# Rotary halves exchanged by transfers between on-chip buffers instead of a permutation product on TensorE

## The chip, the cores and the metric

The kernel runs on one core of a Trainium2 chip. The metric is the device time in microseconds of one execution. All inputs and the output are float32.

## The reference, cut to what matters

A two-layer encoder trunk over 512 frames of width 1024: multi-head latent attention (8 heads) with a gated ConvFFN, then an S5 state-space layer with a gated ConvFFN, and a final RMSNorm. The change concerns the rotary part of the attention only. The key has one rotary piece of 64 channels for all heads, the queries have one for each head. Each is split into halves of 32 channels and turned:

```python
def apply_rope(x, cos, sin):
    xf = x.astype(jnp.float32)
    x1, x2 = jnp.split(xf, 2, axis=-1)
    return jnp.concatenate([x1 * cos - x2 * sin, x1 * sin + x2 * cos], axis=-1).astype(x.dtype)
```

So every channel is multiplied by a cosine, its partner 32 channels away by plus or minus a sine, and the two are added.

## The kernel before, in words

**Layout.** Channels lie along the 128 partitions, the 512 frames along the free axis. A weight matrix is streamed in blocks of 128 output columns through two raw buffers (RAW) and split into a high and a low part (WH by ScalarE, `hi(b)`, L505; WL by VectorE, `lo(b)`, L862), so that each product is three matmuls (L1507 to L1509; L1649 to L1651 for values). Blocks are numbered: 0 to 5 the latent projection, 6 to 9 keys and values (ukv), 10 to 15 queries (uq), 16 to 23 the output projection (wo).

**Transfers of weights.** SyncE issues `load(b)` (L382 to L389) in order of b. `load(b)` first waits until `lo(b-2)` has read the raw buffer that it fills. SyncE's queue is in order, so everything written behind a load waits with it.

**Units.** The keys, values and queries are made in 28 units (`project(u)`, L1632), each a 128x512 tile in a bank of PSUM. Units 0 to 15 are key and value parts, 16 to 27 the queries in the order of QUNITS (L88): 16, 19, 22 and 25 hold rotary channels of two heads each, the others the plain channels of one head. Before a unit starts, its bank must have been read (`unit_free`, L1622; banks in UNIT_BANK, L91): unit 22 waits for the VectorE reading of unit 18, unit 25 for that of 21, unit 27 for that of 24. The readings are `unit_hi(u)` on ScalarE (L586) and, for keys and plain query units, `unit_lo(u)` on VectorE (L991).

**Rotation.** There are five turns, k = 0 for the key and 1 to 4 for the query pairs. The unturned tile lies in RAWR (the key's written by VectorE at L1017, a query pair's by ScalarE at L600). TensorE multiplies it by the signed permutation PERM (`permute(k)`, L1662 to L1670), and VectorE's `turned(k)` (L994) multiplies the product by SIN into TMP (L996), RAWR by COS (L997), and adds (L999). ScalarE then rounds the result (`key_rope_hi` L602, `rope_hi` L606) and VectorE takes the rest (`rope_lo` L1007). COS and SIN are spread over the partitions by `spread(0)` and `spread(1)` (TensorE L1589, ScalarE L541).

**Order.** The order of each engine is written out by hand. On TensorE, permute(0) stands between units 9 and 10, permute(1) to (3) behind units 17, 20 and 23, and permute(4) behind the scores of step 5 in the attention (L1743). VectorE's order around the turns (L1033 to L1049) is: unit_lo(12), turned(0), unit_lo(14), the key's rest, lo(11), lo(12), lo(13); unit_lo(17), turned(1), unit_lo(18), rope_lo(0); lo(14), unit_lo(20), turned(2), unit_lo(21), lo(15), rope_lo(1); unit_lo(23), turned(3), unit_lo(24); and then row_max(0), the attention's first step, with turned(4) in its step 10. The attention has 32 steps (8 heads by 4 query blocks): scores (TensorE), row_max (VectorE), exps (ScalarE), normalize (VectorE), turn (a transpose on TensorE), and pt_copy (ScalarE). ScalarE's exps(0) stands behind unit_hi(25), rope_hi(2) and hi(17).

Of the kernel before, what the change touches and what calls it, by code (L numbers as in the profile page):

```python
# [22 lines left out]
P = 128  # L23
# [30 lines left out]
ALU = mybir.AluOpType  # L54
ACT = mybir.ActivationFunctionType
# [15 lines left out]
FIRST = {}  # L71
# [18 lines left out]
NUNITS = 2 * HEADS + len(QUNITS)  # L90
UNIT_BANK = [(0, 1, 5)[_u % 3] for _u in range(18)] + [(4, 0, 1, 5)[_u % 4] for _u in range(8)] + [0, 1]  # L91

TURN_BANK = (6, 7, 6, 7, 1)


def unit_kind(u):
    if u < 2 * HEADS:
# [4 lines left out]
UNIT_READ = {}  # L102
# [56 lines left out]
for _b in FFN0:  # L159
    _p = PHASE_OF[_b]  # L160
    _rest = FIRST[_p] + BLOCKS[_p] - _b
    _ops = 3 if _p in ("dn00", "dn01") else 2 if _p == "dn02" else 0 if _rest <= 2 else 1
    OPS_AT[_b] = range(_i, min(_i + _ops, MAT_OPS * NJ))
    _i = OPS_AT[_b].stop
    for _o in OPS_AT[_b]:
        if _o % MAT_OPS == MAT_OPS // 2 - 1:
            SPILL_AT[_b + 5] = ("O", _o // MAT_OPS)
        if _o % MAT_OPS == MAT_OPS - 1:
            _n = max(_b + 3, FIRST["up00"])
            while _n - FIRST[PHASE_OF[_n]] < 2:  # L170
                _n += 1
            MAT_AT[_n] = _o // MAT_OPS
            SPILL_AT[_n + 6] = ("K", _o // MAT_OPS)
PLACE_FREE = {3: 1, 5: 2, 7: 4}
LAGS_AT = {1: 4, 3: 3, 4: 5, 6: 7}
assert _i == MAT_OPS * NJ and len(MAT_AT) == NJ and len(SPILL_AT) == 2 * NJ
# [5 lines left out]
def build(nc, d):  # L182
    ctx = ExitStack()
    with ctx:
# [8 lines left out]
        def keep(name, shape, dt=F32):  # L193
            t, base[0] = place(name, shape, dt, base[0])
            return t

        def sem(name):
            return ctx.enter_context(nc.semaphore(name))
# [15 lines left out]
        SQ = [keep(f"SQ{i}", [P, S]) for i in range(2)]  # L214
        DIAG = keep("DIAG", [P, TT, P])
        IDENT = keep("IDENT", [P, P])
        PERM = keep("PERM", [P, P])
        ONES = keep("ONES", [P, P])
        GAIN = keep("GAIN", [P, 5 * KD + KQ + KKV])
        CONV = keep("CONV", [P, DEPTH * 2 * NF, 4])  # L220
# [9 lines left out]
        DCOL = keep("DCOL", [P, KD])  # L230
# [27 lines left out]
        RAWR = [place(f"RAWR{i}", [P, S], F32, ah_at + 2048 * (5 + i))[0] for i in range(3)]  # L258
        TMP, COS, SIN = (place(n, [P, S], F32, al_at + 2048 * (5 + i))[0] for i, n in enumerate(("TMP", "COS", "SIN")))
        SEL, at = place("SEL", [P, TT, P], F32, ql_at)  # L260
# [68 lines left out]
        bank = [ctx.enter_context(nc.psum_tensor(f"bank{i}", [P, S], F32)) for i in range(8)]  # L329
# [7 lines left out]
        s_hi, s_lo, s_mm, s_ev = sem("w_hi"), sem("w_lo"), sem("block_done"), sem("bank_read")  # L337
# [4 lines left out]
        s_par, s_tab, s_pos, s_const = sem("gain_loaded"), sem("tables_loaded"), sem("pos_loaded"), sem("const_made")  # L342
        s_sml, s_ang, s_trig = sem("lambda_loaded"), sem("angles"), sem("trig")
        s_ra, s_cs, s_sel, s_csc = sem("rotary_angles"), sem("rotary_trig"), sem("trig_spread"), sem("trig_copied")
        s_tv, s_fb, s_un, s_uh = sem("latent_squares"), sem("factor_copied"), sem("unit_done"), sem("unit_hi")
        s_read = {"kq": sem("kq_read"), "v": sem("v_read"), "r": sem("rope_read")}
        s_rq, s_rh, s_qr = sem("rope_turned"), sem("rope_hi"), sem("rope_halves")
        s_den, s_b, s_bb, s_neg = sem("ssm_den"), sem("B_loaded"), sem("B_made"), sem("C_negated")
        s_pm, s_rot = sem("permuted"), sem("rotated")
        s_sc, s_mx, s_p, s_pn, s_pt, s_ptc, s_pv = (sem(n) for n in (  # L350
            "scores", "row_max", "exps", "probs", "probs_t", "probs_t_copied", "pv"))
        s_c, s_cv, s_sg, s_h = (sem(n) for n in ("tap2", "conv", "gate", "hidden"))
# [28 lines left out]
        def _(sp):  # L381
            def load(b):  # L382
                if b >= NBLOCKS:
                    return
                name = PHASE_OF[b]
                if b >= RW:
                    sp.wait_ge(s_lo, b - RW + 1)
                n = UNITS[name] * P
                sp.dma_start(RAW[b % RW][:, :n], d["w_" + name][b - FIRST[name]]).then_inc(s_raw[b % RW], 16)  # L389
# [11 lines left out]
            sp.dma_start(INV[:], d["inv"]).then_inc(s_pos, 16)  # L401
            for n in ("lr", "li", "ld"):
                sp.dma_start(small[n][:], d[n]).then_inc(s_sml, 16)
            for t, n in ((IDENT, "ident"), (SEL, "sel"), (PERM, "perm"), (CONV, "conv"), (DCOL, "dcol")):
                sp.dma_start(t[:], d[n]).then_inc(s_tab, 16)
            load(3)
            for t, n in ((CRE, "cre"), (CIN, "cim"), (MASK, "mask")):
# [6 lines left out]
            def lags(j):  # L414
                sp.wait_ge(s_kt, j + 1)
                sp.dma_start(KD_[j], KT[:]).then_inc(s_kw, 16)

            for b in range(4, FIRST["win"] + 4):
                load(b)
                if b == FIRST["wo"] + 5:  # L420
                    sp.wait_ge(s_pv, HEADS)
                    for t, n in ((BRE, "bre"), (BIM, "bim")):
                        sp.dma_start(t[:], d[n]).then_inc(s_b, 16)
                if b in SPILL_AT:
                    what, j = SPILL_AT[b]
                    if what == "O":
                        spill(j)
                    else:
                        lags(j)
# [63 lines left out]
        def _(act):  # L493
            act_ = nc.scalar.activation
# [45 lines left out]

            def spread(n, dst):  # L541
                act.wait_ge(s_sel, n + 1)
                act_(dst[:], bank[4][:], ACT.Copy).then_inc(s_csc, 1)

            hi(0)
            act.wait_ge(s_par, 16)
# [142 lines left out]
                if n == 4 * HEADS + 1:  # L689
                    o_hi(HEADS - 2)  # L690
            o_hi(HEADS - 1)
            act.wait_ge(s_tab, 16 * 5)

            def next_tile(key, kind, j, b):
                act.wait_ge(s_ev, nth(b))
# [144 lines left out]
            for i in range(KD):  # L840
                b = FIRST["glu"] + 2 * i + 1
# [12 lines left out]
        def _(dve):  # L854
            v = nc.vector
# [40 lines left out]

            v.memset(ONES[:], 1.0)
            v.memset(EPST[:], EPS)
            v.memset(WARM[:], 0.0).then_inc(s_const, 1)
            v.memset(KR2[0][64:128, :].bitcast(F32), 0.0)  # L900
            v.memset(KR2[1][0:64, :].bitcast(F32), 0.0)
# [52 lines left out]

            dve.wait_ge(s_sq, KD + KKV)
            v.tensor_tensor(SSKV[:], SQ[0][:], SQ[1][:], ALU.add).then_inc(s_ss, 2)
            dve.wait_ge(s_tab, 16 * 5)
            rstd_cols("x", RX)
            lo(4)
            dve.wait_ge(s_pos, 16 * 5)  # L960
# [31 lines left out]
                                ALU.subtract).then_inc(s_read["kq"], 1)  # L992

            def turned(k):  # L994
                dve.wait_ge(s_pm, k + 1)
                v.tensor_tensor(TMP[:], bank[TURN_BANK[k]][:], SIN[:], ALU.mult).then_inc(s_rot, 1)  # L996
                v.tensor_tensor(RAWR[k % 3][:], RAWR[k % 3][:], COS[:], ALU.mult)  # L997
                v.drain()
                v.tensor_tensor(RAWR[k % 3][:], RAWR[k % 3][:], TMP[:], ALU.add).then_inc(s_rq, 1)  # L999
# [501 lines left out]
        def _(pe):  # L1501
# [85 lines left out]
                    m.then_inc(s_mm, 1)  # L1587

            def spread(n):  # L1589
                pe.wait_ge(s_tab, 16 * 5)  # L1590
                pe.wait_ge(s_cs, n + 1)
                pe.wait_ge(s_ev, WA_READ[4])
                if n == 1:
                    pe.wait_ge(s_csc, 1)
                for c in range(TT):
                    m = mm(bank[4][:, c * P:(c + 1) * P], SEL[:, c, :], TRIG[n][:], start=True, stop=True)
                m.then_inc(s_sel, 1)
# [61 lines left out]
                        m = unit(b, KQ * (c % 2) + k, AH, AL, KKV + k, k == 0, k == KQ - 1, out)  # L1659
                m.then_inc(s_un, 1)  # L1660

            def permute(k):  # L1662
                pe.wait_ge(s_ev, (4, 5, 6, 6, 6)[k])
                if k >= 1:
                    pe.wait_ge(s_read["r"], k)
                if k in (2, 3):
                    pe.wait_ge(s_rot, k - 1)
                if k == 4:
                    pe.wait_ge(s_read["kq"], UNIT_READ[27][1])
                mm(bank[TURN_BANK[k]][:], PERM[:], RAWR[k % 3][:], start=True, stop=True).then_inc(s_pm, 1)  # L1670

            project(0)
            project(1)
            pe.wait_ge(s_fb, 2)
# [2 lines left out]
                project(u)  # L1677
            spread(0)
            project(9)
            permute(0)  # L1680
            project(10)
            spread(1)
            for u in range(11, 2 * HEADS):
# [1 line left out]
            for r in range(3):  # L1685
                project(2 * HEADS + 3 * r)
                project(2 * HEADS + 3 * r + 1)
                permute(r + 1)
                project(2 * HEADS + 3 * r + 2)
            project(25)  # L1690

# [20 lines left out]
            def turn(n):  # L1712
                qb = n % 4
                if n == 0:
                    pe.wait_ge(s_rot, 4)
                    pe.wait_ge(s_read["r"], UNIT_READ[25][1])
                pe.wait_ge(s_pn, n + 1)
                if n >= 3:
                    pe.wait_ge(s_ptc, n - 2)
                for kb in range(qb + 1):  # L1720
                    m = nc.tensor.transpose(bank[5 + n % 3][:, kb * P:(kb + 1) * P],
                                            PR_[qb][:, kb * P:(kb + 1) * P], IDENT[:])
                m.then_inc(s_pt, 1)

            def pv(h):
                pe.wait_ge(s_ptc, 4 * h + 4)
                if h == 0:
                    pe.wait_ge(s_read["v"], 2 * TT)
                if h == 1:
                    pe.wait_ge(s_rot, 5)  # L1730
                if h >= 2:
                    pe.wait_ge(s_act, TILE0["o"] + h - 1)
                for kb in range(TT):
                    m = mm(bank[h % 2][:, kb * P:], V[:, kb, h * VH:(h + 1) * VH], PT[h % 2][:, kb, kb * P:],
                           start=(kb == 0), stop=(kb == TT - 1))
                m.then_inc(s_pv, 1)

            pe.wait_ge(s_ev, 6)
            for n in range(4 * HEADS):
                scores(n)  # L1740
                if n in (0, 1):
                    project(26 + n)
                if n == 5:  # L1743
                    permute(4)
                if n >= 3:
                    turn(n - 3)
                if n >= 9 and n % 4 == 1:
                    pv((n - 9) // 4)
# [233 lines left out]
```

## Time and profile before

| what | value |
|---|---|
| median of 3 runs | 1143.05 us (1139.31 to 1145.65) |
| the profiled execution's own time | 1146.58 us |
| its span in the profile | 1144.8 us |
| mean granted TensorE clock | 0.987 |
| TensorE (PE) busy | 1116.7 us, 98% |
| VectorE (DVE) busy | 788.6 us, 69% |
| ScalarE (ACT) busy | 476.4 us, 42% |

The page of the profile gives busy times for the engines, the chain of work that ended last, the costliest groups of instructions, and the transfers with their time from issue to landing. In the timeline a matmul's start is exact and its end is modelled, so what a matmul costs is read from one start to the next. Positions are us from the start of the span. A table by stretch gives for each stretch its length, then busy us (and instructions) of PE, PEld (TensorE's weight loads), DVE, ACT and POOL, the granted TensorE clock (1.00 is full), the transfer engines' busy share, and GB/s. SPq is SyncE's sequencer, which issues transfers.

### The profile page before, as it was taken

How to read it: one execution, taken by the hardware profiler on the slowest of the kernel's cores; microseconds unless marked ns; L12 is line 12 of the kernel's file. 1: busy time of each engine (PE TensorE's matmuls, PEld its weight loads, DVE VectorE, ACT ScalarE, POOL GpSimd, SP SyncE). 2: the span in 40 equal slices, each digit the busy share in tenths (PEclk: the TensorE clock that was granted, in tenths of full speed). 3: DMA queues.
4: the chain of work that ended last, by engine and by line, in shares of the span. 5: the costliest groups of instructions: out<-in, count | busy, mean ns of one | idle time of the engine just before them, and what ended most of it. 6: DMA issues, size and time to landing. Idle time of an engine off the chain costs nothing.

```text
span 1144.8 us, 14849 instructions
## 1 busy us (share of the span) xinstructions
PE 1116.7 (98%) x5678; PEld 919.5 (80%) x5678; DVE 788.6 (69%) x1202; ACT 476.4 (42%) x721; POOL 57.9 (5%) x154
## 2 busy tenths in 40 slices
PE   8999899999999999999998999999999999999996
PEld 5787778888888888888887887888888888888885
DVE  6657857688787788978855885546765477635665
ACT  5556554455423543345451324334442244423442
POOL 3072004000000000000000000000000000000000
PEclk8999999999999999999998999999999999999998
DMA  6311103233343332433376663332333223232222
GB/s 210 102 59 52 37 20 111 78 114 126 106 130 111 116 123 92 148 111 120 89 260 202 175 186 93 94 109 75 109 95 108 93 92 95 90 111 92 93 78 87
DMA packets 62966, 125.68 MB, mean 110 GB/s; under 512 B 21808, under 2 KB 32560, under 8 KB 62896
## 3 DMA queue, kind: packets, MB, share of 16 engines
q1 hardware_dynamic: 61744, 120.54, 33.4%
q0 software_dynamic: 1152, 4.19, 1.1%
q8 instruction: 45, 0.74, 0.3%
q14 instruction: 25, 0.20, 0.1%
HBM read 110.04 MB, written 14.68 MB: 109 GB/s over the span
## 4 chain that ended last, share of the span: by engine, by line
PE 87%; DVE 5%; DMA 3%; DVEq 2%; ACT 1%; issue 1%; SPq 0%; ACTq 0%
PE bank L1507 27%; PE bank L1509 27%; PE bank L1508 27%; DVE MX L1057 1%; PE bank L1850 1%; DVE P L1065 1%; DVEq L1056 1%; PE bank L1799 1%; PE bank L1842 1%; DMA RAW<-in_w_wa 1%; ACT WH L505 1%; DMA RAW<-in_w_glu 1%; DVE WL L862 1%; DVE X L1289 1%; DMA ud_scratch<-UB 0%
## 5 line engine op out<-in xcount | busy, mean ns | idle before, releaser
L505 ACT ACTIVATE WH<-RAW 128x1024 fp32r<-128x1024 f32 (+1 forms) x184 | 190.0, 1034 | 392.2 <-PE bank L1509 352.6
L1507 PE MATMUL bank<-GH,WH 128*128 128x512 f32 x816 | 323.1, 396 | 3.2 <-DVE GL L920 3.2
L1508 PE MATMUL bank<-GL,WH 128*128 128x512 f32 x816 | 319.6, 392 | 0.0
L1509 PE MATMUL bank<-GH,WL 128*128 128x512 f32 x816 | 319.5, 392 | 0.0
L862 DVE TENSOR_TENSOR WL<-RAW,WH 128x1024 fp32r<-128x1024 f32 (+1 forms) x184 | 219.1, 1191 | 54.4 <-ACT WH L505 53.7
L1507 PE MATMUL bank<-AH,WH 128*128 128x512 f32 x596 | 235.2, 395 | 1.9 <-DVE WL L862 1.1
L1509 PE MATMUL bank<-AH,WL 128*128 128x512 f32 x596 | 232.2, 390 | 0.0
L1508 PE MATMUL bank<-AL,WH 128*128 128x512 f32 x596 | 232.0, 389 | 0.0
L1507 PEld LDWEIGHTS bank<-GH,WH 128*128 128x128 f32 x816 | 154.5, 189 | 36.7 <-DVE GL L920 4.1
L1509 PEld LDWEIGHTS bank<-GH,WL 128*128 128x128 f32 x816 | 154.5, 189 | 32.6
L1508 PEld LDWEIGHTS bank<-GL,WH 128*128 128x128 f32 x816 | 154.6, 189 | 32.4 <-issue 0.7
L1507 PEld LDWEIGHTS bank<-AH,WH 128*128 128x128 f32 x596 | 111.9, 188 | 27.2 <-DVE WL L862 1.5
L1508 PEld LDWEIGHTS bank<-AL,WH 128*128 128x128 f32 x596 | 111.9, 188 | 23.6 <-issue 1.0
L1509 PEld LDWEIGHTS bank<-AH,WL 128*128 128x128 f32 x596 | 111.9, 188 | 23.5
L771 ACT ACTIVATE CV<-Z,CONV 128x512 f32<-128x512 f32 x88 | 71.9, 817 | 94.0 <-DVE HH L1224 56.6
L1242 DVE SCALAR_TENSOR_TENSOR CV<-Z,CONV,CV 128x512 f32<-128x512 f32 x88 | 65.9, 749 | 41.6 <-ACT CV L771 41.6
L1235 DVE TENSOR_TENSOR Z<-bank,RSTD 128x512 f32<-128x512 f32 x88 | 60.5, 687 | 42.9 <-PE bank L1509 41.9
L1105 DVE TENSOR_TENSOR X<-bank,X 128x512 f32<-128x512 f32 x55 | 37.9, 688 | 58.0 <-PE bank L1509 58.0
L1245 DVE SCALAR_TENSOR_TENSOR CV<-Z,CONV,CV 128x512 f32<-128x512 f32 x88 | 66.1, 752 | 6.9 <-issue 0.4
L1228 DVE TENSOR_TENSOR AL<-HH,AH 128x512 fp32r<-128x512 f32 x44 | 30.2, 686 | 4.2 <-ACT AH L758 4.2
L754 ACT ACTIVATE SG<-CV 128x512 f32<-128x512 f32 x44 | 27.2, 618 | 12.1 <-DVE CV L1245 12.1
L1224 DVE TENSOR_TENSOR HH<-SG,CV 128x512 f32<-128x512 f32 x44 | 30.1, 685 | 0.2 <-ACT SG L754 0.2
(270 smaller groups left out, 930.9 us busy)
## 6 DMA issues: line engine op xcount, KB each, us to landing
RAW<-in_w_up SPq DMA_DIRECT2D x88, 512.0 KB, 3.5
RAW<-in_w_dn SPq DMA_DIRECT2D x32, 512.0 KB, 3.5
RAW<-in_w_glu SPq DMA_DIRECT2D x16, 512.0 KB, 3.5
RAW<-in_w_dn SPq DMA_DIRECT2D x16, 384.0 KB, 3.0
RAW<-in_w_wo SPq DMA_DIRECT2D x8, 512.0 KB, 3.5
od_scratch<-OO SPq DMA_DIRECT2D x8, 512.0 KB, 3.7
kd_scratch<-KT SPq DMA_DIRECT2D x8, 512.0 KB, 4.9
O<-od_scratch POOLq DMA_DIRECT2D x8, 512.0 KB, 4.5
```

Of the source, the lines that this page charges most:

```text
L505: act_(WH[b % RH][:, :n], RAW[b % RW][:, :n], ACT.Copy).then_inc(s_hi, 1)
L771: act_(CV[p][:], Z[p][:, 2:S + 2], ACT.Identity, scale=CONV[:, c, 2:3], bias=CONV[:, c, 3:4]).then_inc(s_c, 1)
L862: v.tensor_tensor(WL[b % RH][:, :n], RAW[b % RW][:, :n], WH[b % RH][:, :n].bitcast(F32), ALU.subtract).then_inc(s_lo, 1)
L1105: v.tensor_tensor(X[:, j, :], bank[BANK[b]][:], X[:, j, :], ALU.add).then_inc(s_ev, 1)
L1224: v.tensor_tensor(HH[:], SG[:], CV[0][:], ALU.mult).then_inc(s_h, 1)
L1228: v.tensor_tensor(AL[:, i, :], HH[:], AH[:, i, :].bitcast(F32), ALU.subtract).then_inc(s_act, 1)
L1235: v.tensor_tensor(Z[p][:, 2:S + 2], bank[BANK[b]][:], RSTD[:], ALU.mult).then_inc(s_ev, 1)
L1242: v.scalar_tensor_tensor(out=CV[p][:], in0=Z[p][:, 1:S + 1], scalar=CONV[:, c, 1:2], in1=CV[p][:], op0=ALU.mult, op1=ALU.add)
L1245: m = v.scalar_tensor_tensor(out=CV[p][:], in0=Z[p][:, 0:S], scalar=CONV[:, c, 0:1], in1=CV[p][:], op0=ALU.mult, op1=ALU.add)
L1507: mm(out, wh, hi_[:, k, :], start=start, stop=False)
L1508: mm(out, wh, lo_[:, k, :], start=False, stop=False)
L1509: return mm(out, wl, hi_[:, k, :], start=False, stop=stop)
```

## The change

PERM, its load and `permute` go. Instead SyncE exchanges the halves: `swap(k)` issues four transfers of 32 partitions by 512 elements (64 KB each) from RAWR to TMP, and VectorE's `turned(k)` waits for all four and multiplies TMP by SIN in place. The minus sign that PERM carried is put into SIN: `spread(1)` copies with a scale per partition from a new tile SIGN, filled by four memsets. `swap(0)` is issued behind load(12), `swap(1)` behind load(15), `swap(2)` behind load(16), `swap(3)` and `swap(4)` behind load(17). A swap waits until its RAWR is written and until the turn before it has ended with TMP. The scheduling waits that hung on the old semaphores are replaced by equivalent ones.

```diff
-TURN_BANK = (6, 7, 6, 7, 1)
+SWAP_AT = {FIRST["uq"] + 2: (0,), FIRST["uq"] + 5: (1,), FIRST["wo"]: (2,), FIRST["wo"] + 1: (3, 4)}
...
-        PERM = keep("PERM", [P, P])
+        SIGN = keep("SIGN", [P, 1])
...
+            def swap(k):
+                sp.wait_ge(s_ev, 6)
+                if k >= 1:
+                    sp.wait_ge(s_read["r"], k)
+                    sp.wait_ge(s_rq, k)
+                for r0 in range(0, P, 32):
+                    r1 = r0 + 32 if r0 % 64 == 0 else r0 - 32
+                    sp.dma_start(TMP[r0:r0 + 32, :], RAWR[k % 3][r1:r1 + 32, :]).then_inc(s_swp, 16)
+
             for b in range(4, FIRST["win"] + 4):
                 load(b)
+                if b in SWAP_AT:
+                    for k in SWAP_AT[b]:
+                        swap(k)
...
-                act_(dst[:], bank[4][:], ACT.Copy).then_inc(s_csc, 1)
+                if n == 0:
+                    act_(dst[:], bank[4][:], ACT.Copy).then_inc(s_csc, 1)
+                else:
+                    act_(dst[:], bank[4][:], ACT.Identity, scale=SIGN[:, 0:1]).then_inc(s_csc, 1)
...
+            for r0 in range(0, P, 32):
+                v.memset(SIGN[r0:r0 + 32, :], -1.0 if r0 % 64 == 0 else 1.0)
             v.memset(WARM[:], 0.0).then_inc(s_const, 1)
...
             def turned(k):
-                dve.wait_ge(s_pm, k + 1)
-                v.tensor_tensor(TMP[:], bank[TURN_BANK[k]][:], SIN[:], ALU.mult).then_inc(s_rot, 1)
+                dve.wait_ge(s_swp, 64 * (k + 1))
+                v.tensor_tensor(TMP[:], TMP[:], SIN[:], ALU.mult)
                 v.tensor_tensor(RAWR[k % 3][:], RAWR[k % 3][:], COS[:], ALU.mult)
...
-            def permute(k):
-                pe.wait_ge(s_ev, (4, 5, 6, 6, 6)[k])
...
-                mm(bank[TURN_BANK[k]][:], PERM[:], RAWR[k % 3][:], start=True, stop=True).then_inc(s_pm, 1)
...
-            permute(0)
...
-                permute(r + 1)
...
                 if n == 0:
-                    pe.wait_ge(s_rot, 4)
...
                 if h == 0:
                     pe.wait_ge(s_read["v"], 2 * TT)
+                    pe.wait_ge(s_read["kq"], UNIT_READ[26][1])
                 if h == 1:
-                    pe.wait_ge(s_rot, 5)
+                    pe.wait_ge(s_read["kq"], UNIT_READ[27][1])
...
-                if n == 5:
-                    permute(4)
```

## Rows read from the trace of the kernel before

**Rows 1.** The page: busy times, and the chain that ended last by engine

```profile
PE 1116.7 (98%) x5678; PEld 919.5 (80%) x5678; DVE 788.6 (69%) x1202; ACT 476.4 (42%) x721; POOL 57.9 (5%) x154
...
PE 87%; DVE 5%; DMA 3%; DVEq 2%; ACT 1%; issue 1%; SPq 0%; ACTq 0%
```

**Rows 2.** Table by stretch: projections with turns 1 to 3, then the attention's start

```profile
81.00:101.00 20.00, 20.00 (x85) 15.44 (x84) 15.97 (x24) 10.68 (x16) 9.97 (x24) 1.00 0.37 113
108.00:130.00 22.00, 18.52 (x99) 14.54 (x98) 17.70 (x56) 12.94 (x40) 0.00 (x0) 0.92 0.00 1
```

**Rows 3.** TensorE in order of time: start, us, around permute(1) and permute(4)

```profile
81.60 0.39 PE L1509 MATMUL bank<-AH,WL 128*128 128x512 f32 x1
81.83 1.02 PE L1670 MATMUL bank<-RAWR,PERM 128*128 128x512 f32 x2
...
82.92 0.40 PE L1508 MATMUL bank<-AL,WH 128*128 128x512 f32 x1
...
110.62 0.44 PE L1721 MATMUL bank<-IDENT,P 128*128 128x128 f32 x2 [1.61 <-DVE P L1065]
...
111.66 1.91 PE L1670 MATMUL bank<-RAWR,PERM 128*128 128x512 f32 x2
113.36 0.85 PE L1721 MATMUL bank<-IDENT,P 128*128 128x128 f32 x3
```

**Rows 4.** VectorE in order of time: the turns and what stands between them

```profile
75.18 0.68 DVE L996 TENSOR_TENSOR TMP<-bank,SIN 128x512 f32<-128x512 f32 x1
...
85.34 0.96 DVE L862 TENSOR_TENSOR WL<-RAW,WH 128x768 fp32r<-128x768 f32 x1 [2.95 <-ACT WH L505]
...
86.81 0.68 DVE L996 TENSOR_TENSOR TMP<-bank,SIN 128x512 f32<-128x512 f32 x1
...
88.17 0.69 DVE L999 TENSOR_TENSOR RAWR<-RAWR,TMP 128x512 f32<-128x512 f32 x1
...
93.09 0.68 DVE L996 TENSOR_TENSOR TMP<-bank,SIN 128x512 f32<-128x512 f32 x1
...
98.66 0.68 DVE L996 TENSOR_TENSOR TMP<-bank,SIN 128x512 f32<-128x512 f32 x1
...
101.63 0.11 DVE L1055 MEMSET bank<- 64x64 f32 x1 [0.33 <-PE bank L1710]
```

**Rows 5.** SyncE's queue in order of time: load(12), load(15), load(16), load(17), then spacing

```profile
68.42 0.33 SPq L389 DMA_DIRECT2D RAW<-in_w_uq  x1
...
86.32 0.33 SPq L389 DMA_DIRECT2D RAW<-in_w_uq  x1
...
92.60 0.33 SPq L389 DMA_DIRECT2D RAW<-in_w_wo  x1
...
96.63 0.33 SPq L389 DMA_DIRECT2D RAW<-in_w_wo  x1
...
7.91 1.99 SPq L400 DMA_DIRECT2D POSI<-in_pos  x4
```

**Rows 6.** Transfers by line: count, KB each, median us from issue to landing

```profile
out<-X SPq DMA_DIRECT2D x8, 256.0 KB, 2.3
PERM<-in_perm SPq DMA_DIRECT2D x1, 64.0 KB, 2.8
YB<-yd_scratch SPq DMA_DIRECT2D x8, 256.0 KB, 3.4
```

**Rows 7.** ScalarE in order of time: before the attention's first exponential

```profile
101.57 0.62 ACT L609 ACTIVATE QRS<-RAWR 64x512 fp32r<-64x512 f32 x1
...
105.22 0.37 ACT L654 ACTIVATE P<-bank,MX 128x128 f32<-128x128 f32 x1
```

**Rows 8.** Table by stretch: two stretches behind stalls of TensorE

```profile
111.30:114.70 3.40, 3.40 (x12) 2.26 (x11) 2.49 (x11) 2.39 (x9) 0.00 (x0) 0.50 0.03 7
...
618.40:626.70 8.30, 8.29 (x43) 7.21 (x44) 7.47 (x12) 2.40 (x5) 0.53 (x1) 0.50 0.55 162
```

**Rows 9.** TensorE in order of time: the stall ahead of the second stretch

```profile
618.41 1.97 PE L1850 MATMUL bank<-XR,O 64*128 64x64 f32 x16 [4.12 <-DVE XI L1340]
```

More of the change, by code:

```diff
@@ L348, in build @@
         s_den, s_b, s_bb, s_neg = sem("ssm_den"), sem("B_loaded"), sem("B_made"), sem("C_negated")
-        s_pm, s_rot = sem("permuted"), sem("rotated")
+        s_swp = sem("halves_swapped")
         s_sc, s_mx, s_p, s_pn, s_pt, s_ptc, s_pv = (sem(n) for n in (
@@ L403, in _ @@
                 sp.dma_start(small[n][:], d[n]).then_inc(s_sml, 16)
-            for t, n in ((IDENT, "ident"), (SEL, "sel"), (PERM, "perm"), (CONV, "conv"), (DCOL, "dcol")):
+            for t, n in ((IDENT, "ident"), (SEL, "sel"), (CONV, "conv"), (DCOL, "dcol")):
                 sp.dma_start(t[:], d[n]).then_inc(s_tab, 16)
@@ L691, in _ @@
             o_hi(HEADS - 1)
-            act.wait_ge(s_tab, 16 * 5)
+            act.wait_ge(s_tab, 16 * 4)
             def next_tile(key, kind, j, b):
@@ L956, in _ @@
             v.tensor_tensor(SSKV[:], SQ[0][:], SQ[1][:], ALU.add).then_inc(s_ss, 2)
-            dve.wait_ge(s_tab, 16 * 5)
+            dve.wait_ge(s_tab, 16 * 4)
             rstd_cols("x", RX)
@@ L1589, in spread @@
             def spread(n):
-                pe.wait_ge(s_tab, 16 * 5)
+                pe.wait_ge(s_tab, 16 * 4)
                 pe.wait_ge(s_cs, n + 1)
@@ L1660, in project @@
                 m.then_inc(s_un, 1)
-            def permute(k):
-                pe.wait_ge(s_ev, (4, 5, 6, 6, 6)[k])
[L1664 to L1669, printed above, removed]
-                mm(bank[TURN_BANK[k]][:], PERM[:], RAWR[k % 3][:], start=True, stop=True).then_inc(s_pm, 1)
             project(0)
@@ L1931 @@
     put("ident", np.eye(P, dtype=np.float32))
-    perm = np.zeros((P, P), np.float32)
-    for r in range(P):
-        o = r % 64
-        perm[r + 32 if o < 32 else r - 32, r] = -1.0 if o < 32 else 1.0
-    put("perm", perm)
     put("sel", (np.arange(P)[:, None, None] == np.arange(TT)[None, :, None] * 32 + np.arange(P)[None, None, :] % 32
```

## The prediction

> **What bounds the kernel now.** I read the page first: TensorE is busy 98% of the span and holds 87% of the chain that ended last [rows 1]. So a product taken off TensorE is worth its time only where TensorE has no gaps. The table by stretch shows which stage that is: from 81 to 101 us, where turns 1 to 3 stand, TensorE is busy 20.00 of 20.00 us, while from 108 to 130, in the attention, it is busy 18.52 of 22.00 and VectorE's 17.70 sets the pace [rows 2]. But from 85.34 to 101.2 VectorE is hardly idle either: its rows follow each other to the attention's first step at 101.63 [rows 4]. Two engines are nearly full here, and the change gives to one of them and puts a wait on the other.
>
> The sum is made against the profiled execution, 1146.58 us; the median of the runs is 1143.05. A difference of 0.5%, 5.7 us, is about what a measurement can tell from no change.
>
> **What is removed.** Permute(1) starts at 81.83 and the second matmul behind it at 82.92; with one ordinary matmul's 0.23 (81.60 to 81.83) taken off, it costs 0.86 us [rows 3]. Permutes 0 to 3 all stand in such a gapless stretch, so TensorE can be 0.87, 1.7, 2.6 and 3.4 us earlier, as far as nobody holds it up. Permute(4) takes 1.70 us (111.66 to 113.36), because the granted clock is half there [rows 3, 8], behind a stall of 1.61 us [rows 3]. It stands in the attention. What its removal returns there is between 0.3 us (VectorE sets the pace, and the product fills a gap) and 2.6 us (itself, and all the rest of what half clock costs in that stretch of 3.40 us, 1.7 us with the product's own 0.8). I take 1.9, since TensorE is busy all 3.40 us of it [rows 8]. The load of PERM stands far ahead of its use: nothing.
>
> **What is added at no cost.** The four memsets of SIGN delay the warm-up products by some 0.4 us; the first real products wait for inputs anyway. The copy to SIN stays one instruction, only with a scale, and turned(0), which needs it first, begins at 75.18, when units 10 to 13 have passed since. The product with SIN now reads TMP instead of a bank of PSUM; L999, which reads nothing from PSUM, took 0.69 us against 0.68 [rows 4]. Without these covers they would cost under 1 us together. Swap(0) is issued behind load(12), 68.42 [rows 5]; by the path below it lands at 73.0, and turned(0) is due at 75.18 - 0.87 = 74.3 [rows 4]: hidden, by 1.3 us. Swap(4) follows swap(3) by some 5 us and is used ten steps into the attention: hidden.
>
> **The path of a swap.** Four transfers, each a command for SyncE. POSI's four, also 32 partitions each, start (1.99 - 0.43) / 3 = 0.52 us apart, 0.43 being one of them [rows 5]. A load before it takes 0.40. From issue to landing no row shows a transfer from SBUF to SBUF. The nearest: 2.3 us (256 KB out of SBUF), 2.8 (64 KB from HBM, PERM itself), 3.4 (256 KB, read back) [rows 6]. I take 2.6, between the one that shares its source and the one that shares its size, and 2.3 and 3.4 as ends. So from the issue of the load ahead to VectorE seeing the data: 0.40 + 3 x 0.52 + 2.6 + 0.04 = 4.60 us.
>
> The Trainium skill ("DMA: Bandwidth & Descriptors", Anatomy of one DMA) gives about 2.0 us plus the bytes over 436 GB/s, 2.15 us for 64 KB, and says that the receipt from HBM is the slow part. An estimate by that page would lower the sum below by 3 x 0.45, to about +7.2. The rows here show nothing as short.
>
> **Where it is late.** The swaps stand in SyncE's queue behind loads, and load(b) is released by lo(b-2) on VectorE, which stands just ahead of the very turn that wants the swap. Load(15) is issued at 86.32 and turned(1) starts at 86.81, 0.49 later; load(16) 92.60 and turned(2) 93.09, 0.49 again; load(17) 96.63 and turned(3) 98.66, 2.03 later [rows 4, 5]. VectorE works in order, so it waits each time for the rest of 4.60 us:
> - turned(1): 4.60 - 0.49 = 4.11
> - turned(2): 4.60 - 0.49 = 4.11, because lo(14), behind turned(1), moves with it
> - turned(3): 4.60 - 2.03 = 2.57
>
> Together 10.8 us. VectorE's chain begins 0.87 earlier, since its step before followed TensorE, so turned(3) starts at 98.66 + 10.8 - 0.87 = 108.6. It takes 88.17 - 86.81 + 0.69 = 2.05 us [rows 4] and ends at 110.6. Behind it on VectorE are unit_lo(24) and the attention's first maximum; on ScalarE rope_hi(2), now at 101.57, and the first exponential, 3.65 later [rows 7]. ScalarE's part begins at 110.67 instead, so the attention starts **9.1 us later**. Three waits of TensorE follow from the same delays: unit 22 needs unit_lo(18), which ends at 86.81 + 4.11 - 0.87 + 2.05 + 0.7 = 92.8, while TensorE is there, 2.6 earlier than before, at 89.2 (stall 3.6). Worked out in the same way, unit 25 needs unit_lo(21), 103.1 (stall 4.2), and unit 27 needs unit_lo(24), 111.2 (2.8). The four products gained, 3.4 us, only make these stalls longer. They are not to be subtracted again.
>
> **The clock.** Stalls of 1.61 and 4.12 us had stretches of half clock, 3.4 us and 8.3 us of work, behind them [rows 3, 8, 9]. After these stalls I expect the same. Units 22 to 24 (27 matmuls of 0.23, 6.2 us) have 4 us of slack, so half clock there is nearly free. Half clock over units 25, 26 and the scores of steps 0 and 1 (5.3 us) can cost 2.5, and over the attention's first steps 1 to 3. Bounds 0 and 3.5; I take 1.3, somewhat below what the stretch of before costs.
>
> **Sum.** 9.1 - 1.9 + 1.3 = +8.5 us, so 1155.1 against the profiled 1146.58, and against the median **1151.5 us**. By its bounds: landing 2.3 to 3.4 (-0.9 to +2.4), spacing 0.40 as for a load (-1.1), permute(4) 0.3 to 2.6 and clock 0 to 3.5; not all at one end together, +5 to +13.5.
>
> **Rivals.**
> - *The clock stays half* from the first stall into the attention. Units 22 to 24 then run from 92.8 to 105.0, units 25, 26 and scores to 115.6; unit 27 starts 11.5 us late and is itself 2 longer; less 1.9 with the removed product, about +12, 1155. For it: 8.3 us in one stretch behind a stall of 4.12 [rows 8, 9], and three stalls here. Against: the stretch behind 1.61 was short. Chance 0.12.
> - *Short landing*: SBUF to SBUF in 1.5 us, below every row, and no half clock. Three waits lose 1.1 each: 9.1 - 3.3 - 1.9 = +3.9, 1147. For it: no HBM at either end. Against: 256 KB out of SBUF took 2.3. Chance 0.13.
> - *The transfers hide and TensorE's time comes back*: 3.4 for permutes 0 to 3 and 1.9 for permute(4), -5.3, 1137.7, faster. This decides only if a swap is at hand 0.49 us after the load ahead of it; the issue of four commands alone takes 1.6. Only a VectorE with slack that the rows don't show would let it happen. Chance 0.05.
> - That it doesn't do what it says I leave out: no product remains, and SIN carries the sign.
>
> The forecast (the three waits, +5 to +13.5) has 0.70.
>
> **Range and chances.** The forecast's own span, 1148 to 1156.5, is widened to take in the first rival and most of the second, and a microsecond of the measurement: **1146.5 to 1157.5**. Faster: the third rival, 0.05. Within 5.7 us: the short landing and the lowest part of the forecast, 0.17. Slower: 0.78.
>
> **What would show it.** VectorE idle before L996's successor three times, about 4.1, 4.1 and 2.6 us, released by the transfers into TMP, and hardly before turned(0) and turned(4). TensorE idle before units 22, 25 and 27, released by VectorE's L991. Load(16) and load(17) issued some 3 and 7 us later than now. First exponential near 114.3. The clock's table shows whether half clock lies in 90 to 120. I am wrong if VectorE's waits are below 1 us, if TensorE has no stall before unit 22, or if the attention starts late and a later stage takes it back.

## The result, and the profile after

The changed kernel took 1151.1 us (median of 4, 1149.98 to 1151.87) against 1142.24 us (median of 4), a ratio of 1.0078 with a 95% interval from 1.0060 to 1.0095: 8.9 us slower. The forecast was 1151.5, and +8.5 against the median known then, 1143.05; a fourth execution has since moved that median.

The page of the changed kernel, to be read beside [rows 1]:

```profile
PE 1114.6 (97%) x5668; PEld 919.1 (80%) x5668; DVE 789.0 (69%) x1206; ACT 476.7 (41%) x721; POOL 59.5 (5%) x154
...
PE 85%; DVE 6%; DMA 4%; DVEq 2%; ACT 1%; issue 1%; SPq 1%; ACTq 0%
```

TensorE has 2.1 us less work and a smaller share of a longer span. In the chain that ended last, VectorE, the transfers and SyncE's queue each have a point more.

VectorE in order of time, in the stage of the turns (beside [rows 4]). In brackets stands the idle time before an instruction, and what ended it:

```profile
79.31 0.97 DVE L876 TENSOR_TENSOR WL<-RAW,WH 128x768 fp32r<-128x768 f32 x1 [3.08 <-ACT WH L516]
80.20 0.68 DVE L1007 TENSOR_TENSOR QL<-bank,QH 128x512 fp32r<-128x512 f32 x1
84.68 0.69 DVE L1012 TENSOR_TENSOR TMP<-TMP,SIN 128x512 f32<-128x512 f32 x1 [3.80 <-DMA TMP<-RAWR]
...
95.64 0.69 DVE L1012 TENSOR_TENSOR TMP<-TMP,SIN 128x512 f32<-128x512 f32 x1 [4.53 <-DMA TMP<-RAWR]
...
104.27 0.69 DVE L1012 TENSOR_TENSOR TMP<-TMP,SIN 128x512 f32<-128x512 f32 x1 [2.96 <-DMA TMP<-RAWR]
```

Three waits, 11.3 us together, each ended by the transfers into TMP. The turns 0 (68.97) and 4 (127.16) start with no such wait. TensorE's stalls that follow from them, before units 22, 25 and 27:

```profile
87.46 0.50 PE L1523 MATMUL bank<-AH,WH 128*128 128x512 f32 x1 [3.51 <-DVE QL L1007]
...
98.36 0.80 PE L1523 MATMUL bank<-AH,WH 128*128 128x512 f32 x1 [2.87 <-DVE QL L1007]
...
106.98 0.50 PE L1523 MATMUL bank<-AH,WH 128*128 128x512 f32 x1 [1.60 <-DVE QL L1007]
```

SyncE's queue (beside [rows 5]): the weight load, and the four commands of a swap behind it.

```profile
80.31 0.33 SPq L388 DMA_DIRECT2D RAW<-in_w_uq  x1
80.76 2.42 SPq L424 DMA_DIRECT2D TMP<-RAWR  x4
90.55 0.33 SPq L388 DMA_DIRECT2D RAW<-in_w_wo  x1
90.99 2.41 SPq L424 DMA_DIRECT2D TMP<-RAWR  x4
99.20 0.33 SPq L388 DMA_DIRECT2D RAW<-in_w_wo  x1
```

Transfers by line (beside [rows 6]):

```profile
TMP<-RAWR SPq DMA_DIRECT2D x20, 64.0 KB, 2.6
```

From the issue of the load to VectorE's start the path is 84.68 - 80.31 = 4.37 us for turn 1, and 5.09 and 5.07 for turns 2 and 3. A single command takes 0.59 us, so they start (2.42 - 0.59) / 3 = 0.61 us apart.

**How the two profiles compare.** The profiled execution of before was a slow one: its fifth weight block is split 5 us later than in the changed kernel's, before anything that the change touches. So I compare stretches between two instructions that both kernels have. One is VectorE's split of the fifth weight block, `lo(4)`, ahead of all turns. The other is row_max(31), the attention's last. For before and for the changed kernel:

```profile
33.36 1.22 DVE L862 TENSOR_TENSOR WL<-RAW,WH 128x1024 fp32r<-128x1024 f32 x1
...
101.81 0.29 DVE L1057 TENSOR_REDUCE MX<-bank 128x1 f32<-128x128 f32 x1
...
161.60 0.69 DVE L1057 TENSOR_REDUCE MX<-bank 128x1 f32<-128x512 f32 x1
```

```profile
28.05 1.22 DVE L876 TENSOR_TENSOR WL<-RAW,WH 128x1024 fp32r<-128x1024 f32 x1
...
107.12 0.29 DVE L1073 TENSOR_REDUCE MX<-bank 128x1 f32<-128x128 f32 x1
...
165.40 0.69 DVE L1073 TENSOR_REDUCE MX<-bank 128x1 f32<-128x512 f32 x1
```

The stretch is 128.2 us before and 137.3 after: +9.1 us. Between lo(13) and row_max(0) alone it is +11.3 us (16.5 before, 27.8 after), as much as the three waits; 0.7 us come back ahead of lo(13) and 1.5 us behind row_max(0). The same stretches, from each run's timeline, in us (the runs are told below; the last column is the ratio of times to before, measured with each run):

| run | lo(4) at | lo(4) to row_max(31) | lo(13) to row_max(0) | ratio, 95% interval |
|---|---|---|---|---|
| before | 33.4 | 128.2 | 16.5 | 1 |
| before_again | 30.1 | 126.8 | 16.3 | 1.0002 (0.9989 to 1.0016) |
| changed | 28.1 | 137.3 | 27.8 | 1.0078 (1.0060 to 1.0095) |
| first_ahead | 28.2 | 135.1 | 24.2 | 1.0072 (1.0058 to 1.0087) |
| later_ahead | 28.1 | 130.1 | 20.5 | 1.0030 (1.0018 to 1.0042) |
| all_ahead | 31.9 | 127.5 | 16.8 | 1.0009 (0.9999 to 1.0018) |
| no_exchange | 28.0 | 126.4 | 16.6 | 1.0000 (0.9989 to 1.0011) |
| fill | 28.1 | 137.3 | 27.6 | 1.0082 (1.0060 to 1.0104) |
| eight_commands | 28.4 | 144.2 | 33.6 | 1.0144 (1.0111 to 1.0177) |
| best_order | 28.1 | 128.5 | 19.8 | 1.0010 (0.9996 to 1.0024) |
| before_lo | 28.7 | 128.2 | 17.5 | 1.0004 (0.9995 to 1.0014) |
| ahead_fill | 28.8 | 128.0 | 17.1 | 1.0000 (0.9990 to 1.0011) |
| ahead_lo | 28.8 | 125.1 | 17.0 | 0.9991 (0.9979 to 1.0003) |
| ahead_lo_again | 31.8 | 126.2 | 17.0 | 0.9983 (0.9970 to 0.9996) |

### The profile page after: what moved, and what is told of

Read it like the earlier page. It is cut to its first block, busy times and chain, and to the rows that moved or that the text cites. A ratio compares the mean times of both kernels' runs of the same rounds, so it can differ in the third digit from the quotient of the medians.

```text
span 1150.1 us, 14852 instructions
## 1 busy us (share of the span) xinstructions
PE 1114.6 (97%) x5668; PEld 919.1 (80%) x5668; DVE 789.0 (69%) x1206; ACT 476.7 (41%) x721; POOL 59.5 (5%) x154
## 4 chain that ended last, share of the span: by engine, by line
PE 85%; DVE 6%; DMA 4%; DVEq 2%; ACT 1%; issue 1%; SPq 1%; ACTq 0%
PE bank L1523 26%; PE bank L1525 26%; PE bank L1524 26%; DVE MX L1073 1%; PE bank L1852 1%; DVE WL L876 1%; DVE P L1081 1%; DMA ud_scratch<-UB 1%; PE bank L1801 1%; DMA TMP<-RAWR 1%; PE bank L1844 1%; ACT WH L516 1%; PE bank L1738 1%; DMA RAW<-in_w_glu 1%; DVE X L1305 1%
## 5 line engine op out<-in xcount | busy, mean ns | idle before, releaser
L1244 DVE TENSOR_TENSOR AL<-HH,AH 128x512 fp32r<-128x512 f32 x44 | 30.1, 685 | 4.2 <-ACT AH L772 4.2
L1240 DVE TENSOR_TENSOR HH<-SG,CV 128x512 f32<-128x512 f32 x44 | 30.1, 685 | 0.1
```

Source lines behind the costliest of these rows:

```text
L1240: v.tensor_tensor(HH[:], SG[:], CV[0][:], ALU.mult).then_inc(s_h, 1)
L1244: v.tensor_tensor(AL[:, i, :], HH[:], AH[:, i, :].bitcast(F32), ALU.subtract).then_inc(s_act, 1)
```

## The experiments

The theory: the loss is VectorE's three waits, and they are there because each swap stands in SyncE's queue behind a weight load that is released just ahead of the turn. The rivals: transfers and loads hinder each other, or half clock behind TensorE's stalls carries part of the loss.

**Swaps 1 to 3 one load earlier** (changed kernel, 11 executions).

```diff
-SWAP_AT = {FIRST["uq"] + 2: (0,), FIRST["uq"] + 5: (1,), FIRST["wo"]: (2,), FIRST["wo"] + 1: (3, 4)}
+SWAP_AT = {FIRST["uq"] + 2: (0,), FIRST["uq"] + 3: (1,), FIRST["uq"] + 5: (2,), FIRST["wo"]: (3,), FIRST["wo"] + 1: (4,)}
```

> The changed kernel with swap(1), swap(2) and swap(3) issued one load earlier (behind load(13), load(15) and load(16)), swap(4) behind load(17); nothing else changes. Theory (the loss is three waits of VectorE, because each swap stands in SyncE's queue behind a load that is released just ahead of the turn): VectorE's waits for the transfers fall from 3.8, 4.5 and 3.0 us to below 0.2, 0.2 and about 0.6, TensorE's stalls before units 22 and 25 go, and the time falls by 10 to 12 us against the changed kernel, to 1 to 4 us below the kernel before, 1138 to 1142. Rival (transfers and weight loads get in each other's way, wherever they stand in the queue, and the half clock behind the stalls carries part of the loss): the weight loads land later instead, and at least 4 us of the loss stay, 1146 or more.

Measured: 1141.93 us, ratio 1.0009 (0.9999 to 1.0018). The loss is gone: the time is 9.2 us below the changed kernel's. I had expected 10 to 12, and a time below the kernel before, which it isn't. VectorE waits before the turns only once:

```profile
98.02 0.69 DVE L1012 TENSOR_TENSOR TMP<-TMP,SIN 128x512 f32<-128x512 f32 x1 [0.37 <-DMA TMP<-RAWR]
```

TensorE's stall before unit 22 is down to 0.31 us, and those before units 25 and 27 are gone. The one wait that is longer than before is that of lo(13), for which the changed kernel waited 3.08 us:

```profile
84.03 0.96 DVE L876 TENSOR_TENSOR WL<-RAW,WH 128x768 fp32r<-128x768 f32 x1 [3.97 <-ACT WH L516]
```

Swap(1)'s four transfers are issued right behind load(13), and the block lands later. From the issue of load(13) to ScalarE's hi(13), here and in the run ahead_fill below, which differs only in the attention:

```profile
79.15 0.34 SPq L388 DMA_DIRECT2D RAW<-in_w_uq  x1
83.15 0.85 ACT L516 ACTIVATE WH<-RAW 128x768 fp32r<-128x768 f32 x1 [2.91 <-DMA RAW<-in_w_uq]
```

```profile
76.03 0.34 SPq L388 DMA_DIRECT2D RAW<-in_w_uq  x1
79.36 0.85 ACT L516 ACTIVATE WH<-RAW 128x768 fp32r<-128x768 f32 x1 [2.23 <-DMA RAW<-in_w_uq]
```

That is 4.0 us here and 3.3 there. It is 3.8 in first_ahead, 3.3 in both runs of ahead_lo, and 3.0 to 3.2 in the nine profiles in which no swap follows load(13). So the rival is right about 0.2 to 0.9 us of ten, and how much it is varies between executions of the same order.

**No exchange at all** (changed kernel, 12 executions; the rotary channels are multiplied by the sine without being exchanged).

```diff
-                if b in SWAP_AT:
-                    for k in SWAP_AT[b]:
-                        swap(k)
...
-                dve.wait_ge(s_swp, 64 * (k + 1))
-                v.tensor_tensor(TMP[:], TMP[:], SIN[:], ALU.mult)
+                if k >= 1:
+                    dve.wait_ge(s_read["r"], k)
+                v.tensor_tensor(TMP[:], RAWR[k % 3][:], SIN[:], ALU.mult)
```

> The changed kernel without the exchange: no swaps are issued, and turned(k) multiplies RAWR itself by SIN into TMP, so the rotary channels are not exchanged. It shows what the removed products are worth if their replacement costs nothing. Theory (3.4 us for permutes 0 to 3 on a full TensorE, and 0.3 to 2.6 us for permute(4)): 3.7 to 6 us below the kernel before, about 1137.5. Rival (VectorE, nearly full in this stage, is the bound, and the freed time of TensorE only lengthens its waits): less than 1.5 us below the kernel before.

Measured: 1141.4 us, ratio 1.0000 (0.9989 to 1.0011). The rival's answer: the removed products are worth less than 1.3 us, even if their replacement is free. VectorE's timeline shows why:

```profile
79.20 0.99 DVE L873 TENSOR_TENSOR WL<-RAW,WH 128x768 fp32r<-128x768 f32 x1 [3.06 <-ACT WH L513]
80.11 0.68 DVE L1004 TENSOR_TENSOR QL<-bank,QH 128x512 fp32r<-128x512 f32 x1
80.71 0.79 DVE L1010 TENSOR_TENSOR TMP<-RAWR,SIN 128x512 f32<-128x512 f32 x1
```

From lo(11) over load(13) to lo(13), and then through VectorE's full queue, runs a chain of its own: lo(11) to row_max(0) is 21.6 us here and 21.3 in both profiles of before. So TensorE, 20.00 of 20.00 us busy in [rows 2], was about as tight as that chain, and no tighter.

**The first swap alone, and the later two alone** (changed kernel, 4 and 9 executions).

```diff
+SWAP_AT = {FIRST["uq"] + 2: (0,), FIRST["uq"] + 3: (1,), FIRST["wo"]: (2,), FIRST["wo"] + 1: (3, 4)}
```

> The changed kernel with swap(1) alone issued earlier, behind load(13); swap(2) and swap(3) stay behind load(16) and load(17). Theory: the first wait of 3.8 us goes, the waits of 4.5 and 3.0 stay as long as they were; the time is 3.5 to 4.5 us below the changed kernel, 1146.5 to 1148. Rival (the slack ahead of the later turns is used up by the first wait, so that its removal comes back as longer later waits): within 1.5 us of the changed kernel.

```diff
+SWAP_AT = {FIRST["uq"] + 2: (0,), FIRST["uq"] + 5: (1, 2), FIRST["wo"]: (3,), FIRST["wo"] + 1: (4,)}
```

> The changed kernel with swap(2) and swap(3) issued earlier, behind load(15) and load(16); swap(1) stays behind load(15). Theory: the first wait stays at 3.8 us, the second falls to nearly nothing and the third to about 0.6; the time is 6 to 8 us below the changed kernel, 1143 to 1145. With the run that moves swap(1) alone the two savings add up to that of the run that moves all three, within 1.5 us. Rival (half clock behind the first stall is what makes the later ones long): a wait stays before turned(2) of over 2 us.

Measured: 1149.34 and 1144.79 us. The waits before the turns in the first run, and then in the second:

```profile
92.65 0.69 DVE L1012 TENSOR_TENSOR TMP<-TMP,SIN 128x512 f32<-128x512 f32 x1 [4.56 <-DMA TMP<-RAWR]
101.47 0.69 DVE L1012 TENSOR_TENSOR TMP<-TMP,SIN 128x512 f32<-128x512 f32 x1 [3.15 <-DMA TMP<-RAWR]
```

```profile
84.67 0.69 DVE L1012 TENSOR_TENSOR TMP<-TMP,SIN 128x512 f32<-128x512 f32 x1 [3.73 <-DMA TMP<-RAWR]
...
97.05 0.69 DVE L1012 TENSOR_TENSOR TMP<-TMP,SIN 128x512 f32<-128x512 f32 x1 [0.36 <-DMA TMP<-RAWR]
```

The waits behave as the theory says: each goes when its own swap moves, and the others stay. Between lo(13) and row_max(0) the first run saves 3.6 us and the second 7.3, together 10.9 of the 11.0 that moving all three saves. In the time, the second gives 6.3 us, as expected, and the first only 1.8 by the medians, half of what I expected (3.5 to 4.5). By its profile, 0.7 us of the difference is load(13), which lands later as in all_ahead, and 0.7 is the attention (59.0 us from row_max(0) to row_max(31) instead of 58.3), whose cause stays open. The 0.4 that are left are less than the intervals.

**The stalls of TensorE filled** (changed kernel, 6 executions).

```diff
+            def fill(n):
+                for _ in range(n):
+                    mm(bank[6][:], ONES[:], X[:, 0, :], start=True, stop=True)
...
+                if r == 2:
+                    fill(3)
...
+            fill(3)
             project(25)
...
+                    if n == 1:
+                        fill(1)
                     project(26 + n)
```

> The changed kernel with idle products on TensorE: three in float32 (0.86 us each) ahead of unit 22, three ahead of unit 25 and one ahead of unit 27, into a bank that nobody reads, so that TensorE is busy in most of its stalls. Theory (VectorE's waits set the time, and the stalls' half clock falls where TensorE has slack): within 1.5 us of the changed kernel, 1149.5 to 1151.5. Rival (half clock behind the stalls carries 2 us or more of the loss): 1148.5 or less, with no half clock between 85 and 105 us.

Measured: 1151.23 us. The changed kernel had these three stretches of half clock:

```profile
88.00:91.40 3.40, 3.40 (x9) 2.63 (x8) 2.93 (x4) 2.13 (x5) 0.00 (x0) 0.51 0.00 0
98.20:101.60 3.40, 3.24 (x8) 2.56 (x9) 3.03 (x5) 2.93 (x5) 0.00 (x0) 0.50 0.36 101
115.30:118.70 3.40, 3.28 (x14) 3.28 (x15) 2.93 (x12) 2.55 (x10) 0.00 (x0) 0.50 0.01 2
```

With the stalls filled the first two are gone, the third is there (115.5 to 118.9), and lo(4) to row_max(31) is 137.3 us in both. Half clock where TensorE waits for VectorE anyway costs nothing. The idle products don't fill the stalls to the end: 0.86, 1.83 and 1.71 us remain, the second of them here:

```profile
98.31 0.53 PE L1523 MATMUL bank<-AH,WH 128*128 128x512 f32 x1 [1.83 <-DVE QL L1007]
```

No half clock follows the last two, while it followed a stall of 1.61 us in [rows 3] and [rows 8]. The length of a stall alone doesn't decide it.

**Eight commands instead of four** (changed kernel, 4 executions).

```diff
-                for r0 in range(0, P, 32):
-                    r1 = r0 + 32 if r0 % 64 == 0 else r0 - 32
-                    sp.dma_start(TMP[r0:r0 + 32, :], RAWR[k % 3][r1:r1 + 32, :]).then_inc(s_swp, 16)
+                for r0 in range(0, P, 16):
+                    r1 = r0 + 32 if r0 % 64 < 32 else r0 - 32
+                    sp.dma_start(TMP[r0:r0 + 16, :], RAWR[k % 3][r1:r1 + 16, :]).then_inc(s_swp, 16)
...
-                dve.wait_ge(s_swp, 64 * (k + 1))
+                dve.wait_ge(s_swp, 128 * (k + 1))
```

> The changed kernel with each exchange issued as eight transfers of 16 partitions instead of four of 32. Bytes are the same, and four more commands stand in SyncE's queue per swap. Theory (the path of a swap is serial, and each command costs 0.63 us in it): each of the three waits grows by 2.5 us, and the time by 6.5 to 8.5 us against the changed kernel, 1157.5 to 1160. Rival (the landing of the bytes behind the weight load sets the wait, and the commands are hidden by it): the waits grow by less than 1 us each, 1154 or less.

Measured: 1157.52 us, ratio 1.0144. The waits:

```profile
70.26 0.69 DVE L1012 TENSOR_TENSOR TMP<-TMP,SIN 128x512 f32<-128x512 f32 x1 [0.88 <-DMA TMP<-RAWR]
88.39 0.69 DVE L1012 TENSOR_TENSOR TMP<-TMP,SIN 128x512 f32<-128x512 f32 x1 [6.20 <-DMA TMP<-RAWR]
100.98 0.69 DVE L1012 TENSOR_TENSOR TMP<-TMP,SIN 128x512 f32<-128x512 f32 x1 [6.22 <-DMA TMP<-RAWR]
111.29 0.69 DVE L1012 TENSOR_TENSOR TMP<-TMP,SIN 128x512 f32<-128x512 f32 x1 [4.64 <-DMA TMP<-RAWR]
```

They grow by 2.4, 1.7 and 1.7 us, the stretch by 6.9 and the time by 6.4 (expected: 2.5 each, and 6.5 to 8.5). The path is serial in SyncE's commands: in turns 1 to 3 the eight hold its queue for 4.93 us instead of 2.42. In turns 2 and 3 part of that comes back, because the last of eight is issued 2.5 us later behind the 512 KB load and lands in 2.0 us instead of 2.8. Turned(0), hidden in the changed kernel by about 1.6 us, now waits too.

**The kernel before once more** (10 executions, no edit).

> The kernel before, unchanged, profiled and timed once more. The profiled execution of before stood 5 us above the median, with a stall of TensorE of 2.3 us and 6.8 us of half clock at 12 to 19 us, which the profile of the changed kernel doesn't have. If these vary from execution to execution, this profile has them or not, and its execution time moves with them by about 5 us; if they belong to the kernel before, they are there again. The ratio should be 1 within 0.15%.

Measured: 1142.08 us, ratio 1.0002. In this profile lo(4) is at 30.08 instead of 33.36, and the half clock at the start is 3.4 us long instead of 6.8. In the other profiles lo(4) lies between 28.0 and 31.9, whatever the kernel. The start varies from execution to execution by up to 5 us. The half clock in the attention varies too: before had it, before_again not (58.4 us from row_max(0) to row_max(31) instead of 59.8), though TensorE's stall there is 1.61 us long in both.

**In search of a faster version.** Since the chain over load(13) holds the stage, lo(11), which releases it, was moved ahead of the key's rest:

```diff
             unit_lo(14)
-            key_rope_lo()
             lo(11)
+            key_rope_lo()
             lo(12)
```

First with swap(1) behind load(14), to keep it away from load(13) (12 executions):

> The kernel with all swaps ahead (swap(1) now behind load(14) instead of load(13), so that it doesn't stand ahead of load(14) nor beside load(13)), and lo(11) moved ahead of the key's rest on VectorE, so that load(13) is released earlier. Theory (what holds this stage without any wait for a swap is the chain from lo(11) through load(13) to lo(13), on which VectorE idles 3 us): load(13) starts 1.4 us earlier, lo(13) 1.4 to 2.2 earlier, and the time is 1 to 2.5 us below the run with all swaps ahead, 1139.5 to 1141. Rival (TensorE or ScalarE takes over at once): within 0.5 us of that run.

Measured: 1143.39 us, ratio 1.0010, above the 1139.5 to 1141 that I expected. Lo(13) came 1.2 us earlier, but this took its place:

```profile
82.58 0.69 DVE L1012 TENSOR_TENSOR TMP<-TMP,SIN 128x512 f32<-128x512 f32 x1 [2.90 <-DMA TMP<-RAWR]
```

Then with swap(1) behind load(13), as in all_ahead, twice (12 and 13 executions), and the same move in the kernel before (12 executions):

> The kernel with all swaps ahead (swap(1) behind load(13) again, as in the run all_ahead), and lo(11) moved ahead of the key's rest on VectorE. In the run best_order the same move brought lo(13) 1.2 us earlier, but swap(1) behind load(14) landed 2.9 us late. Theory (the chain lo(11), load(13), lo(13) holds this stage): the wait before turned(1) is below 1 us, lo(13) is about 1 us earlier than in all_ahead, and the time is 0.5 to 1.5 us below it, 1140.5 to 1141.5. Rival (swap(1)'s transfers beside load(13) take back what the earlier release gives): within 0.5 us of all_ahead.

> The run ahead_lo once more (all swaps ahead, lo(11) ahead of the key's rest), to see whether it beats the kernel before: it stood at a ratio of 0.9991 with an interval from 0.9979 to 1.0003. If the 1.7 us that its trace shows between the fifth weight split and the last maximum are kept to the end, the ratio is 0.9985 to 0.9995 and both intervals together lie below 1; if it was chance, the ratio is 1.000 or above.

> The kernel before with lo(11) moved ahead of the key's rest on VectorE, and the products kept. It shows whether that chain, and not TensorE, sets the pace of this stage in the kernel before. Theory (it does): lo(13) 1.3 us earlier and the time 0.3 to 1.2 us below the kernel before. Rival (TensorE is full in this stage and is the bound): the same time within 0.3 us, and VectorE waits for units instead.

Measured: 1141.13 and 1140.37 us, ratios 0.9991 (0.9979 to 1.0003) and 0.9983 (0.9970 to 0.9996); in the kernel before 1142.21 us, 1.0004 (0.9995 to 1.0014). So the products off TensorE and the load released earlier bring 1 to 2 us together, of which the second run alone is clear of 1, and each of the two by itself brings nothing that can be measured. In the kernel before TensorE holds what lo(13) gives: lo(13) to row_max(0) grows from 16.3 to 17.5 us, and VectorE's wait for TensorE ahead of row_max(0), 0.33 us in [rows 4], becomes this:

```profile
96.93 0.11 DVE L1055 MEMSET bank<- 64x64 f32 x1 [0.89 <-PE bank L1710]
```

Without the products the chain over load(13) holds the stage.

**The attention's first stalls filled** (all_ahead with two idle products, 12 executions).

```diff
+                if n in (3, 4):
+                    mm(bank[7][:], ONES[:], X[:, 0, :], start=True, stop=True)
                 if n >= 3:
                     turn(n - 3)
```

> The kernel with all swaps ahead plus two idle float32 products on TensorE in the attention, ahead of the first and the second transpose step, where it stands idle 0.9 and 1.7 us, into a bank that nobody reads. Theory (with the products gone, TensorE arrives at the attention earlier, stands idle longer in its first steps, and half clock for 3.4 us follows, which gives back what was gained): no half clock between 100 and 125 us in the profile, and the time 0.7 to 2 us below the run all_ahead, 1140 to 1141.2. Rival (half clock falls there whatever TensorE does, or where it has slack): within 0.5 us of all_ahead.

Measured: 1141.77 us, within 0.2 us of all_ahead. There is no half clock up to 120 us in this profile, but then this:

```profile
120.60:124.00 3.40, 3.40 (x8) 1.76 (x7) 3.17 (x9) 3.34 (x10) 0.00 (x0) 0.50 0.00 0
```

In all_ahead it lies at 109.7 us, and here at 120.6, behind another stall of TensorE (1.75 us). The time is the same. The theory fell: the idle products don't save the half clock.

## Why the prediction was right, point by point

- **Three waits, 4.11, 4.11 and 2.57 us, 10.8 together**: 3.80, 4.53 and 2.96, 11.3 together. The path of 4.60 us was 4.37, 5.09 and 5.07. The landing I took between two rows, 2.6 us, is the median measured; behind the 384 KB load it is 2.1 and behind the 512 KB loads 2.8. That is partly luck, since no row of before showed such a transfer. The commands are 0.61 us apart and not 0.52, and the load ahead takes 0.44 and not 0.40. The Trainium skill ("DMA: Bandwidth & Descriptors", Anatomy of one DMA) would give 2.15 us for a transfer of 64 KB; its formula is fitted to transfers that GpSimd issues, and these are SyncE's, which the prediction doesn't say. The trace agrees with it in turn 1 (2.1 us), and not in turns 2 and 3 behind the larger loads (2.8); the median is 2.0 us in all_ahead.
- **VectorE's chain 0.87 us earlier**: lo(4) to lo(11) shrinks from 47.1 to 46.3 us, -0.84; at lo(13) 0.7 of it is left.
- **The attention starts 9.1 us later.** The first exponential moved from 105.22 [rows 7] to 110.03, and with the 5.3 us by which the starts differ this is +10.1, against before_again too. Of the surplus of 1.0, the longer waits are 0.5; the rest I didn't trace.
- **TensorE's stalls before units 22, 25 and 27, 3.6, 4.2 and 2.8 us**: 3.51, 2.87 and 1.60. All three are there and end with VectorE's reading, but the last two are over a microsecond shorter than worked out. Half clock is the likely reason: 3.4 us of it make TensorE 1.7 us later at unit 25. With it gone (fill) the gap before unit 25 is 4.4 us, 1.83 idle and three idle products of 0.86.
- **Permute(4), -1.9, and the clock, +1.3**: net -0.6, and measured between -1.5 and -0.1. Row_max(0) to row_max(31) took 59.8 us in the profile of before (product and 3.4 us of half clock), 58.4 in before_again (product, no half clock) and 58.3 in the changed kernel's (no product, 3.4 us of half clock). By these three, product and half clock are worth about the same, 1.4 us. But the ten profiles without the product, all with 3.4 us of half clock in the attention (ahead_fill, with its idle products, aside), lie between 58.1 and 59.0, so each value is uncertain by most of a microsecond. That the product's removal is what brought the half clock in is not shown: before and before_lo have both. After the change half clock costs nothing in the stage of the stalls (fill), as I had said for units 22 to 24 but not for 25 and 26; the loss it makes is in the attention.
- **The four products only lengthen the stalls**: right, and more than I saw. I priced the rival in which all transfers hide at -5.3 us. No_exchange and all_ahead show that case: 0.0 and +1.0 us. The step that failed there is that TensorE, busy 20.00 of 20.00 us, gets its time back once the transfers hide. VectorE's chain over load(13), with 2.95 us idle in [rows 4], leaves of it only the 0.8 us gained ahead of lo(11): lo(11) to row_max(0) is no shorter without the products.
- **Swap(0) hidden by 1.3 us**: no wait; with eight commands, 2.5 us later, 0.88, so the margin was 1.6.
- **The memsets, the scaled copy, the product from TMP**: the warm-up starts 0.4 us later, at 2.00 instead of 1.61, and nothing else of it is seen.
- **Base of the sum.** The profiled execution stood 3.5 us above its median mostly because of the 5 us ahead of lo(4). The sum was a difference in a later stage, so it carried over to the median. That +8.5 met +8.9 so closely is in part luck: the attention started 1.0 us later than worked out, and the last two terms gave back up to 0.9 us more. The measured difference is itself known only as 6.9 to 10.9 us, and against before_again the stretch lo(4) to row_max(31) grows by 10.5 us, not 9.1.
- The rivals: the half clock staying on (three separate stretches of 3.4 us instead), the short landing (2.1 us once, 2.8 twice) and the hidden transfers are all refuted for this order. All_ahead makes half of the last true: the transfers hide, but TensorE's time doesn't come back.

## What to carry to other kernels

Ask of a new transfer which instruction stands ahead of it in its queue, and what releases that one; here each stood behind a load that was issued only 0.6 to 2.1 us before the data were due, and one line that moves them a load earlier is worth 9 us. To issue them from another engine's queue, with no load ahead of them, was not tried. Before you count an engine's freed time as a gain, look for a second chain of the same length: an engine with no idle time in its rows is not the only bound when another waits 3 us for a load and is full after that. Compare executions between two instructions that both have, not from the start of the span.

## What the runs showed of the hardware

- A transfer of 64 KB from SBUF to SBUF landed 2.0 to 3.5 us after its issue, 2.6 in the median, though neither end is in HBM (1.9 to 3.9 over all runs, the median 2.0 in all_ahead); a 256 KB write from SBUF to HBM took 2.3 [rows 6].
- A command that moves 32 partitions within SBUF holds SyncE for 0.59 us, one that fetches POSI from HBM 0.43 [rows 5], a 512 KB weight load 0.33. With 16 partitions it is 0.59 again (eight_commands).
- Four transfers issued right behind a 384 KB load delayed its landing by 0.2 us (ahead_fill, ahead_lo), 0.7 (first_ahead) and 0.9 (all_ahead).
- Behind TensorE's stalls of 1.6 to 3.5 us lay 3.4 us of half clock in some places (changed kernel, at 88.0, 98.2 and 115.3 us) and none in others (1.83 and 1.71 us in fill, 1.60 us at 107 us in the changed kernel). It moved when stalls were filled, and was in one profile of the kernel before and not in the other.
